# Extra TensorE products in the waits of a two-block transformer kernel

## The reference, cut to what matters

```
for i in range(2):                                   # first block
    mix = mixer_mla_sb(x, ...) if i == 0 else mixer_fox(x, ...)
    x = layer_norm(ALPHA * x + mix, ln1_g[i], ln1_b[i])
    x = layer_norm(ALPHA * x + swiglu(x, w1[i], w3[i], w2[i]), ln2_g[i], ln2_b[i])
    x = x + sigmoid(x @ ple_w_gate[i] + ple_b_gate[i]) * (p[i] @ ple_w_proj[i])
...
h = modulate(rms_norm(x, g_norm_mix), sh1, sc1)      # second block
x = x + ga1 * (concat(retention(h), sparse_attention(h)) @ w_out)
h = modulate(rms_norm(x, g_norm_ffn), sh2, sc2)
x = x + ga2 * peer(h, ...)
return rms_norm(x, g_norm_final)
```

## Time and profile before

| what | value |
|---|---|
| median of 3 runs | 1870.27 us (1869.08 to 1873.82) |
| profiled execution | 1867.74 us, span of its instructions 1866.4 us |
| mean granted TensorE clock, as a share of full | 0.974 |
| busy shares | PE 94%, DVE 69%, ACT 48%, POOL 12% |
| shares of the chain that ended last | PE 77%, DVE 8%, ACT 5%, issue 4%, DMA 3%, POOL 3% |

### The profile page before, as it was taken

How to read it: one execution, slowest core, us unless ns; L and a number is a source line. 1 busy time by engine, 2 the same in 40 slices (tenths; PEclk the granted TensorE clock), 3 DMA queues, 4 the chain that set the end, 5 groups by cost and what they waited for, 6 DMA issues and landing times.

```text
span 1866.4 us, 31955 instructions
## 1 busy us (share of the span) xinstructions
PE 1751.0 (94%) x11408; PEld 1573.2 (84%) x11408; DVE 1282.6 (69%) x2300; ACT 903.4 (48%) x1584; POOL 231.9 (12%) x147
## 2 busy tenths in 40 slices
PE   7988999989989999898887998999999999999997
PEld 6757998768879987797777998999999998888885
DVE  5376866775768666767655998777786666666665
ACT  4734443455544434546444444777774443333332
POOL 1020000001110000022103799100000000000000
PEclk9989999999999999999988999999999999999999
DMA  7534756644536675444223454444445555555553
GB/s 270 199 112 138 263 180 239 237 158 145 170 119 237 216 255 194 140 147 136 80 90 114 154 173 153 146 143 137 146 138 165 184 186 185 187 186 190 191 184 120
DMA packets 85893, 317.56 MB, mean 170 GB/s; under 512 B 9568, under 2 KB 9840, under 8 KB 85024
## 3 DMA queue, kind: packets, MB, share of 16 engines
q1 hardware_dynamic: 76464, 278.43, 44.6%
q10 hardware_dynamic: 7776, 26.50, 4.0%
q0 software_dynamic: 1552, 11.25, 1.6%
HBM read 315.08 MB, written 1.05 MB: 169 GB/s over the span
## 4 chain that ended last, share of the span: by engine, by line
PE 77%; DVE 8%; ACT 5%; issue 4%; DMA 3%; POOL 3%; POOLq 0%; ACTq 0%; SPq 0%; DVEq 0%
PE bank L253 23%; PE bank L255 22%; PE bank L254 22%; PE bank L2120 3%; POOL wl L208 2%; DVE wl L208 2%; ACT wh L201 2%; DMA ada<-in_w_ada 1%; PE bank L493 1%; DMA ring<-in_stream 1%; PE bank L346 1%; PE bank L563 1%; PE bank L528 1%; DVE ada L334 1%; PE bank L527 0%
## 5 line engine op out<-in xcount | busy, mean ns | idle before, releaser
L201 ACT ACTIVATE wh<-ring 128x1024 fp32r<-128x1024 f32 x529 | 559.0, 1059 | 778.0 <-PE bank L255 702.8
L208 DVE TENSOR_TENSOR wl<-ring,wh 128x1024 fp32r<-128x1024 f32 x477 | 583.8, 1227 | 448.6 <-ACT wh L201 448.5
L253 PE MATMUL bank<-xh,wh 128*128 128x256 f32 x2072 | 599.1, 289 | 14.2 <-POOL wl L208 7.3
L255 PE MATMUL bank<-xh,wl 128*128 128x256 f32 x2072 | 589.3, 284 | 0.0
L254 PE MATMUL bank<-xl,wh 128*128 128x256 f32 x2072 | 589.2, 284 | 0.0
L253 PEld LDWEIGHTS bank<-xh,wh 128*128 128x128 f32 x2072 | 400.7, 193 | 20.7 <-issue 9.1
L254 PEld LDWEIGHTS bank<-xl,wh 128*128 128x128 f32 x2072 | 400.4, 193 | 1.2
L255 PEld LDWEIGHTS bank<-xh,wl 128*128 128x128 f32 x2072 | 399.9, 193 | 0.0
L253 PE MATMUL bank<-wh,wa_high 128*128 128x512 f32 x512 | 202.4, 395 | 2.1 <-DVE weighted L2139 1.4
L255 PE MATMUL bank<-wh,wa_low 128*128 128x512 f32 x512 | 201.9, 394 | 0.0
L254 PE MATMUL bank<-wl,wa_high 128*128 128x512 f32 x512 | 201.9, 394 | 0.0
(11 more groups left out here) (417 smaller groups left out, 2316.0 us busy)
## 6 DMA issues: line engine op xcount, KB each, us to landing
ring<-in_stream SPq DMA_DIRECT2D x529, 512.0 KB, 3.4
ada<-in_w_ada ACTq DMA_DIRECT2D x48, 512.0 KB, 4.4
rows<-in_rows POOLq DMA_DIRECT2D x1, 2560.0 KB, 10.7
con<-in_early POOLq DMA_DIRECT2D x1, 2078.0 KB, 9.1
rows<-in_rows POOLq DMA_DIRECT2D x2, 1024.0 KB, 5.6
x_feature_major<-in_x_fm ACTq DMA_DIRECT2D x4, 256.0 KB, 8.0
x<-in_x_tm POOLq DMA_DIRECT2D x1, 1024.0 KB, 7.9
weighted<-in_subkeys POOLq DMA_DIRECT2D x1, 1024.0 KB, 8.3
```

The lines of the kernel that those rows point to most:

```text
L201: C.activation(wh[q % AHEAD][:, :], ring[slot][:, :], ACT.Copy).then_inc(s_high, 1)
L208: low.tensor_tensor(wl[q % AHEAD][:, :], ring[slot][:, :], wh[q % AHEAD][:, :], ALU.subtract).then_inc(s_low, 1)
L253: T.matmul(o, left[0], right[0], start=start, stop=False, skip_group_check=True)
L255: return T.matmul(o, left[1], right[0], start=False, stop=stop, skip_group_check=True)
```

## The change

A helper `keep_running(b, n)` gives TensorE n products of 128x128 fp32 tables (`ident` as weights, `iota` as data) into a bank that the next real writer clears anyway. It is called at six places: behind the last product of both mixers (19 products each, in `norm1`), at the end of `ple` in layer 0 (9) and layer 1 (16), in `rms_operand(0)` behind the transposes (16), and in `rms_operand(1)` ahead of them (20). While the first loads come, 13 products of 128x256 zeros are run, for which DVE first clears a part of `z`; the first norm waits for them before it writes `z`. Nobody reads the results. Nothing is removed.

```diff
+    def keep_running(b, n):
+
+        for _ in range(n):
+            T.matmul(b[:, 0:P], ident, iota, start=True, stop=True, skip_group_check=True)
+
...
+    zero_set = dve.did(V.memset(z[:, 0, 0:S], 0.0))
     half_set = dve.did(V.memset(nhalf[:, :], -0.5))
+    T.wait_ge(*zero_set)
+    for _ in range(13):
+        idle = T.matmul(bank[7][:, 0:S], z[:, 0, 0:P], z[:, 0, 0:S], start=True, stop=True, skip_group_check=True)
+    idled = pe.did(idle)
     for j in range(KD // 2):
...
         y1 = ple_product(1, p_in)
+        T.wait_ge(*done[1, 0])
+        keep_running(LAST[2] if layer == 0 else LAST[0], 9 if layer == 0 else 16)
         gate_sum(1, 1, y)
...
             dve.wait(later["rows" if layer == 0 else "rows01"])
+            if layer == 0:
+                dve.wait(idled)
+            keep_running(bank[4], 19)
             layer_norm(z, st, first, y, src, bank[4:8], f"ln1_g{layer}", f"ln1_b{layer}", (3,) if layer == 0 else (-1, 3))
...
             n1.append(dve.did(V.tensor_scalar(dst[:, 1, gs], src[:, 1, gs], rr[:, 1:2], None, ALU.mult)))
+        if which:
+            keep_running(banks[0], 20)
         turned = turn_halves(dst, banks, (n0, n0), n1)
+        if not which:
+            keep_running(bank[6], 16)
         shift = 3 * KD if which else 0
```

## The result

The changed kernel takes 1859.12 us (1857.92 to 1861.01, 7 runs) against 1869.08 us (1864.19 to 1876.42, 7 runs) of the kernel before. The profiled execution took 1858.93 us.

The account below looks back on a forecast made before the run. TensorE, busy 94% of the span, was taken as the bound. Gains of 5.8 us less 1.6 gave 4.2, or 1863.5 us from the profiled 1867.74; adding back 1.7 gave 1865.2 us, range 1860 to 1870 for 8 in 10.

Parts of the forecast that it names:

- the waits that I left alone: Waits inside the mixers: the prediction fails as a whole if their own losses change by more than a few us.
- Item 1: Price of one 128-column fill product: taken as 0.11 us at full clock, 0.21 us at half clock.
- the fills fill only half of each wait: At norms and gates: 1.8 to 2.5 us left idle, so one or two of five places still lose the clock.
- the 1.6 us taken off: Deduction for places at norms and gates that still lose the clock, at 1.1 to 1.5 us each.
- Item 2: Fills at norms and gates delay no real work while the wait covers them: cost nothing.
- the rival's point of decision: Rival that fills hold real work up (2%, about 1885 us): a fill would have to cost more than 0.22 us.
- Item 3: Transposes at full clock behind mixers a and c and in both RMS norms: 4.1 us gained if all four hold.
- the loss only moves: Rival, 18%: clock falls during or behind the transposes, products run cold instead; 1870 to 1871 us, no change.
- Item 4: End of the first gate: transposes give about 0.4 us and ten products 0.9, together 1.3 us.
- Item 5: Second fill of `rms_operand(0)`: first products behind it run warmer, 0 to 0.3 us, taken as 0.1.
- Item 6: Start: zero products end by about 6.6 us, then TensorE idles again; 0.3 us taken of 0 to 2.8.
- The 1.7 us added back: Two thirds of the 2.5 us by which the profiled execution lay below the median of the runs shown.

Follow-up runs that it names:

- p1: Kernel before plus 13 products of two columns at the start, with clearing of z and waits, no other fill: 1861.78 us, ratio 0.997.
- p2: Kernel before plus 32 products of two columns at the start, with clearing of z and waits, no other fill: 1864.55 us, ratio 0.9976.
- b1: An unchanged copy of the kernel before, run again for a second trace: 1869.05 us, ratio 1.001.
- g1: Changed kernel with only the fills at the gates' ends and the 16 behind the transposes of `rms_operand(0)`: 1865.21 us, ratio 0.9977 to the kernel before.
- n2: Changed kernel with about half the fills at norms and gates and no start products: 1858.47 us, ratio 0.9953 to the kernel before.
- h1: Changed kernel with about half the fills behind the start, the 13 zero products kept: 1861.1 us, ratio 0.9954 to the kernel before.
- a1: An unchanged copy of the changed kernel, run again: 1859.91 us, ratio 0.9967 to the kernel before.
- a3: An unchanged copy of the changed kernel, run again in a later group: 1860.33 us, ratio 0.9949 to the kernel before.
- n3: Changed kernel with only the two fills of 19 in the norms behind the mixers: 1860.81 us, ratio 0.9971 to the kernel before.
- s1: Changed kernel with only the 13 zero products at the start, no other fill: 1860.01 us, ratio 0.9958 to the kernel before.
- c1: Kernel before with the load of `con` issued at once, no fills and no start products: 1868.93 us, ratio 0.9989.
- s3: Changed kernel with only the clearing of z and TensorE's wait for it, no products or fills: 1868.25 us, ratio 1.0009 to the kernel before.
- s4: Only the 13 zero products at the start, no other fill, run a second time: 1863.24 us, ratio 0.9958 to the kernel before.
- s2: Changed kernel with 6 zero products at the start instead of 13, no other fill: 1865.61 us, ratio 0.9997 to the kernel before.
- n1: Changed kernel with all fills but those at the start, zero products, clearing and waits left out: 1862.63 us, ratio 0.9973 to the kernel before.

## Why the prediction was wrong, point by point

**The sum lacked its largest term.** The prediction named "the waits that I left alone", inside the mixers, as what could overturn it as a whole, and priced them at nothing. Waits that it had left alone did move, but other ones: for a ring piece at 388 us, for the subkeys at 1000, and for a ring piece at 1160. What the traces show to move with them is the place in TensorE's program at which its blocks of instructions are fetched. By p1 and p2 added instructions that do almost no work are worth 5.6 us [2.2, 8.8] and 4.5 us [1.5, 7.5]; in the traces it is 1.7 us at 388, 2.2 us at 1160 in three of the four kernels that add nothing ahead, and 1.9 us at 1000 against b1. It would also explain why the parts don't add up: each part brings instructions, so each carries this gain once, and the start alone (7.8), the mixers' fills alone (5.4) and the half fills (8.8) hold it in common. g1 adds instructions only behind 388, and its trace lacks the first of the three gains.

**Item 1, the price of a fill, was off by a factor of two.** I read `x8` of the earlier trace rows as eight products; it was four. A fill costs 0.22 us: x38 in 4.40 us, and 11 more in 2.46. So "the fills fill only half of each wait", on which the 1.6 us taken off rested, was false. The half-clock price has the same factor of two: 0.21 us is one instruction. What the prediction feared of half-filled waits can be seen in the half fills: with some 2.2 and 2.4 us left idle behind the mixers, the transposes ran partly cold at both in n2 and n4, and at one in h1. The medians show no cost for it.

**Item 2, real work held up.** At 0.22 us the fills just reach the rival's point of decision. At the norms nothing measurable is late. At the first gate's end something is: there the first ScalarE instruction behind the gate is 0.33 us later than in the kernel before, counted from the one at 390 (0.5 and 0.6 in a1 and a3), and within 0.05 us of it in n3, s1, p1 and h1, which have none or four fills there. The fill costs some 0.4 us.

**Item 3, the transposes (4.1 us).** Against b1 the sections give 1.1 us behind mixer a, 0.95 in `rms_operand(0)` and 1.1 in `rms_operand(1)`, 3.1 in all; a1 and a3 agree within 0.4. Behind mixer c nothing is left, as the rival "the loss only moves" had it: transposes warm, products cold from 545.3.

**Item 4, the gate's end (1.3 us).** In g1, where the ring piece is late as in the kernel before, the trace is 1.46 us ahead by the instruction at 402.7, counted from the one at 390, about what was forecast. But c1, which has the piece late and no fill, is 1.45 ahead there, and b1 and s3 0.5, so this isn't shown to be the fill's doing. And n3, s1 and p1, whose piece is not late, keep the clock there without a fill and are 1.2 us ahead, and the changed kernel only 0.9. With its piece on time the fill is worth nothing, and no run shows that it is worth anything otherwise.

**Item 5 (0.1 us)** was 0.55: the products behind `rms_operand(0)` keep their clock. **Item 6, the start (0.3 us).** Its working was wrong, since the zero products end at 9.4 us and not by 6.6, and the first real ones run warm. The trace's answer was nearly right all the same, by luck: 1.38 us ahead at 17.7 us, 0.14 behind at 30 (0.5 ahead of b1), as TensorE waits for `con` until 22.6 and is cold from 23.1. By the ratios s1 and s4 lie 2 to 3 us below p1 and p2, with intervals that overlap.

Together: 3.1 + 0.55 - 0.4 + 0.5, or 3.8 us, from the named items (all against b1) and some 5 from the added instructions make about 9 us, against 10 measured (9.5 in a3 and 6.2 in a1, by ratio). The named items came to less than the 4.2 forecast for them, although the waits were filled wholly; that the time fell within 1 us of the range is no merit of theirs. The 1.7 us added back for the spread between executions led away from the result: seven executions of the changed kernel lie within 3.1 us, seven of the kernel before within 12.2. The sum is a consistency and no proof, as each control is known to some 3 us only.

**A share of the clock that isn't separated.** The granted clock is known for every execution, and the profiled one of before isn't typical: 0.974, where 144 executions beside the experiments have a median of 0.969. The changed kernel has 0.977, the half fills 0.975 to 0.977, p1 and p2 0.9725 and 0.974. Among those 144 executions 0.001 more of clock goes with 1.1 us less, so as an estimate 0.008 more would go with 9 us, about the whole gain. Most executions of the kernel before thus lose the clock at more places, or for longer, than the profiled one, and part of what added instructions do may come that way. It isn't all of it: s4 has the clock of the kernel before (0.970) and is 7.9 us faster.

**Left open.** s2 should carry the gain of position too, and its trace shows it at 388 and 1160, but its median shows none; at the subkeys it still has the packet in the load. n1, with whole fills and no start, gives 5.0 us where half fills give 8.8 and 8.4. That the packet at 386.5 us makes the piece late is read from the traces and from p1 and p2; a fetch wasn't moved by itself, so nothing here separates it from another effect of the program's length. And no version beat the changed kernel: half the fills without the start do the same (0.9953 and 0.9955) with fewer instructions.

## What to carry to other kernels

Work that only keeps TensorE busy pays where a wait stands between dense work and short dependent work, a microsecond each here at three of four norms; half the wait gave the same median here, though the transposes behind the mixers ran cold in part, and a fill longer than the wait is paid in full where the work behind it is on the chain. Count instructions in the trace against the source before pricing one. And before a gain of 0.3% is put down to what an edit does, run the edit's instructions without their work: here this control had half of the gain.

## What the runs showed of the hardware

- A 128-column fp32 product is two instructions of 0.11 us each at full clock; a 128x128 transpose is one.
- Fetching a block of a program goes over the same 16 DMA engines as the data: one packet of 16 KB, 1.28 us on one engine. One 512 KB load took 5.2 us with it in the kernel before, and 3.5 and 3.2 us without it in the changed kernel and p1; a 1 MB load 5.3 to 8.3 us with it in six traces, and 5.1 to 5.3 without it in fourteen.
- One DVE operation on 128x512 fp32 from two tables took 0.68 us alone and 2.9 us beside POOL's split of a piece (three in 8.0 us). The Trainium skill, "SBUF — State Buffer", section "Who interferes with whom", says that only the port pair which both share causes contention and that it is locked exclusively; 2.9 us is about one POOL operation (2.7) and 0.2 more, which agrees.
- A product of two columns takes 0.22 us for each of its instructions at the start (26 in 5.71 us); the weight loads are busy for 5.61 us of it, so they set the step.
